# Order of the value products, the second half of the output projection and the norm's scaling in the cross attention stage of an encoder layer

## What is computed

```python
def cross_attn(h, mem_n, wq, wkv, wo):
    q = (h @ wq).reshape(b, t, X_HEADS, X_HEAD_DIM)
    kv = (mem_n @ wkv).reshape(b, m, 2, X_HEADS, X_HEAD_DIM)
    s = jnp.einsum('bqhd,bkhd->bhqk', q, kv[:, :, 0]).astype(f32) * (X_HEAD_DIM ** -0.5)
    p = jax.nn.softmax(s, axis=-1)
    o = jnp.einsum('bhqk,bkhd->bqhd', p.astype(h.dtype), kv[:, :, 1]).reshape(b, t, X_HEADS * X_HEAD_DIM)
    return o @ wo
...
x = x + cross_attn(rmsnorm(x, norm_cross[l]), mem_n, x_wq[l], x_wkv[l], x_wo[l])
gate, up = jnp.split(rmsnorm(x, norm_ffn[l]) @ ffn_w_gu[l], 2, axis=-1)
x = x + (jax.nn.silu(gate) * up) @ ffn_w_down[l]
```

## Time and profile before

| | |
|---|---|
| median of 3 executions | 1893.69 us (1892.82 to 1894.38) |
| the profiled execution's own time | 1895.65 us |
| its span, first to last instruction | 1893.8 us |
| mean granted TensorE clock | 0.958 of full speed |
| PE busy | 1715.6 us, 91% of the span |
| PEld, DVE, ACT, POOL busy | 76%, 39%, 34%, 29% |
| the chain that ended last | PE 80%, DVE 11%, ACT 5% |

### The profile page before, as it was taken

The page is one execution under the profiler, slowest core; times in us unless marked ns, Lnnn a source line. Parts: engine busy times, 40 slices in busy tenths (PEclk is TensorE's granted clock), DMA queues, the critical chain, the costliest instruction groups (busy, mean ns, idle before and its releaser), DMA issues.

```text
span 1893.8 us, 32570 instructions
## 1 busy us (share of the span) xinstructions
PE 1715.6 (91%) x13937; PEld 1430.3 (76%) x13937; DVE 742.0 (39%) x1219; ACT 651.9 (34%) x1218; POOL 552.5 (29%) x498
## 2 busy tenths in 40 slices
PE   7998988899876982988999899999999999999998
PEld 5886777778654771777998687888888888888886
DVE  3104888333265558455223264131233033213316
ACT  4224887322356432433224374221111121211212
POOL 4222763131025324324225102222222222222220
PEclk9998999899878996899999999999999999999999
DMA  5110000021000000001413101111211111111112
GB/s 186 51 60 1 1 1 1 23 71 42 17 1 6 4 4 0 4 4 47 183 51 96 38 1 46 61 41 44 61 48 48 45 50 51 45 56 45 45 45 95
DMA packets 60176, 81.27 MB, mean 43 GB/s; under 512 B 4610, under 2 KB 47776, under 8 KB 60032
## 3 DMA queue, kind: packets, MB, share of 16 engines
q1 hardware_dynamic: 59088, 76.60, 12.6%
q0 software_dynamic: 944, 2.58, 0.5%
HBM read 74.96 MB, written 4.19 MB: 42 GB/s over the span
## 4 chain that ended last, share of the span: by engine, by line
PE 80%; DVE 11%; ACT 5%; issue 2%; DMA 1%; POOL 1%; SPq 0%; DVEq 0%; ACTq 0%
PE PS L1542 13%; PE PS L1543 12%; PE PS L1545 12%; PE PS L1795 7%; PE PS L2139 4%; PE PS L2138 4%; PE PS L2137 4%; PE PS L1555 3%; PE PS L1557 3%; PE PS L1556 3%; PE PS L1653 3%; PE PS L1687 2%; PE PS L1859 2%; PE PS L1679 1%; PE PS L2058 1%
## 5 line engine op out<-in xcount | busy, mean ns | idle before, releaser
L427 POOL TENSOR_TENSOR WL<-RAW,WH 128x512 fp32r<-128x512 f32 x224 | 307.9, 1385 | 913.8 <-ACT WH L589 913.8
L1542 PE MATMUL PS<-HH,WH 128*128 128x512 f32 x1040 | 406.9, 391 | 9.5 <-POOL WL L427 8.0
L1543 PE MATMUL PS<-HL,WH 128*128 128x512 f32 x1040 | 405.7, 390 | 0.0
L589 ACT ACTIVATE WH<-RAW 128x512 fp32r<-128x512 f32 x224 | 138.9, 631 | 594.6 <-PE PS L1545 297.2
L1545 PE MATMUL PS<-HH,WL 128*128 128x512 f32 x1040 | 321.1, 390 | 0.0
L1542 PEld LDWEIGHTS PS<-HH,WH 128*128 128x128 f32 x1040 | 196.1, 189 | 50.6 <-issue 8.3
L1545 PEld LDWEIGHTS PS<-HH,WL 128*128 128x128 f32 x1040 | 195.8, 188 | 40.8
L1543 PEld LDWEIGHTS PS<-HL,WH 128*128 128x128 f32 x1040 | 196.1, 189 | 40.3
L1492 DVE TENSOR_TENSOR FU<-PS,ACTB 128x512 f32<-128x512 f32 x44 | 27.3, 683 | 456.9 <-PE PS L1545 456.9
L2137 PE MATMUL PS<-WH,AH 128*128 128x512 f32 x352 | 136.9, 389 | 0.0
L2138 PE MATMUL PS<-WL,AH 128*128 128x512 f32 x352 | 136.9, 389 | 0.0
(11 more groups left out here) (319 smaller groups left out, 2802.7 us busy)
## 6 DMA issues: line engine op xcount, KB each, us to landing
RAW<-in_ffn_w_gu SPq DMA_DIRECT2D x88, 256.0 KB, 2.8
RAW<-in_w_in SPq DMA_DIRECT2D x48, 256.0 KB, 2.8
RAW<-in_ffn_w_down SPq DMA_DIRECT2D x44, 256.0 KB, 2.6
XT<-in_x SPq DMA_DIRECT2D x8, 512.0 KB, 4.8
RAW<-in_w_out SPq DMA_DIRECT2D x16, 256.0 KB, 2.7
X<-in_x SPq DMA_DIRECT2D x8, 512.0 KB, 8.2
RAW<-in_x_wkv SPq DMA_DIRECT2D x16, 256.0 KB, 2.7
out_x<-FO SPq DMA_DIRECT2D x8, 512.0 KB, 2.6
```

The lines of the kernel that those rows point to most:

```text
L427: pool.tensor_tensor(w_low, RAW[:, p % NRAW], w_high.bitcast(F32), ALU.subtract).then_inc(w_lo, 1)
L589: act.activation(split_at(p)[0], RAW[:, p % NRAW], ACT.Copy).then_inc(w_hi, 1)
L1542: pe.matmul(where(ct, i), wh[:, k, c], ah(kt)[:, t0:t0 + n], start=first and starts(ct, i), stop=False, skip_group_check=True)
L1543: pe.matmul(where(ct, i), wh[:, k, c], al(kt)[:, t0:t0 + n], start=False, stop=False, skip_group_check=True)
```

## The change

Two orders are changed, and no instruction is added or removed. On the PE, values(qb) moves ahead of wo_half(qb-1, 1). On DVE, scale moves from the end of a step to a place behind the next step's c_row_max (so that step qb scales tile qb-2), and c_second(qb) moves ahead of add_wo(qb-1, 1). The ACT program is the same.

```diff
@@ vector engine @@
             for qb in range(NT + 2):
                 if qb + 1 < NT:
                     c_row_max(qb + 1)
+                if qb >= 2:
+                    scale(n3, qb - 2, lambda tt: X[:, tt], lambda tt: XN2[:, tt % 2], BS, BR, GBF[:, :])
                 if 1 <= qb <= NT:
                     add_wo(qb - 1, 0)
                 if qb + 1 < NT:
...
                 if qb >= 2:
                     norm_lo(n3, qb - 2, lambda tt, b: HH[:, 4 * b:4 * b + 4, tt * P:(tt + 1) * P],
                             lambda tt, b: HL[:, 4 * b:4 * b + 4, tt * P:(tt + 1) * P], bank=lambda tt: 6)
-                if 1 <= qb <= NT:
-                    add_wo(qb - 1, 1)
                 if qb < NT:
                     c_second(qb)
                 if 1 <= qb <= NT:
-                    scale(n3, qb - 1, lambda tt: X[:, tt], lambda tt: XN2[:, tt % 2], BS, BR, GBF[:, :])
+                    add_wo(qb - 1, 1)
@@ tensor engine @@
                     turned(qb)
                 if qb >= 2:
                     ffn_tile(qb - 2)
+                if qb < NT:
+                    values(qb)
                 if qb:
                     wo_half(qb - 1, 1)
-                if qb < NT:
-                    values(qb)
```

## The result

| | before | after |
|---|---|---|
| median of all executions, us | 1895.69 (20) | 1902.41 (20) |
| the profiled execution's own span, us | 1893.8 | 1897.9 |
| scores of tile 0 to the first gate product, us | 103.44 | 108.37 |
| one steady step, us | 11.56 | 12.44 |

The ratio of after to before is 1.0032, with a 95% interval of 1.0019 to 1.0046. That is +6.1 us on the 1895.69 us of before, between +3.6 and +8.7. (It is not the ratio of the two medians, which is 1.0035.) The forecast was +4.9 us, and 1898.6 us for the median.

A forecast was written before the change was run, and what follows sets the result against it. It took the PE to bound the kernel, 10.85 us of work and a 0.71 us hole per step. Five steps of +0.85 (+4.25) and start and end (+0.64) gave +4.9 us, a median of 1898.6 us, range 1896.2 to 1903.3.

The forecast's parts named there:

- (a): DVE: row maxima no longer behind scale, could start when scores end, about 1.9 us after those start, cutting the old loop.
- (b): PE: value products directly behind the transposes need their own tile's CPT copy, making a new loop of 12.41 us.
- the old loop: Value products, OH copy, squares, scale, row maxima, residual add, second half, next value products: 11.56 us, the whole step.
- the hole: PE's idle time before the second half in each step of before: 0.71 us.
- The new loop: Second half, residual add, squares, table loads, exponentials, CPT copy, value products, next second half: 12.41 us a step.
- The price that no row of before had in its place: ACT's exponentials right behind their table load: no gap (0.01 us) at the lower bound.
- Rival 4: Page's drain after ACT's table load is real on the new loop: 5 x 1.38 = +6.9 us more, 1905.5; chance 0.03.
- The edges: Start and end of the cross attention stage, outside the five steady steps: together +0.64 us; gate products at 1170.37.
- Rival 1: ACT reaches the exponentials before stat blocks it: step 11.25 us, -0.9 us, 1892.8; chance 0.05.
- Rival 2: The new loop partly looser, release or copy faster: steps of +0.5 to +0.75, 1896.2 to 1897.4; chance 0.10.
- Rival 3: PE clock falls in the new 1.56 us hole before value products: +1.55 us per fall, 1900.2 to 1906.4; chance 0.12.

The follow-up runs named there:

- e3: Against before, only scale moved behind the next row maxima on DVE; step 10.79 us, ratio 0.9982.
- e4: Changed kernel with the root of the norm ahead of the feed-forward part replaced by a copy on ACT; step 11.26 us, ratio to before 0.9983.
- e6: Changed kernel with the squares of the norm ahead of the feed-forward part done twice on ACT; step 13.54 us.
- e1: Against before, only the PE's part: values(qb) ahead of wo_half(qb-1, 1), DVE's order kept; first step 14.04 us, ratio 1.0089.
- e2: Against before, only DVE's part: scale and c_second moved, PE's order kept; step 11.86 us, ratio 1.0018.
- e7: Changed kernel with c_second put back behind the second residual add; step 12.45 us, executed once.
- e9: Kernel with only scale moved, plus the squares of the norm ahead of the feed-forward part done twice on ACT; step 11.48 us.
- e5: Kernel before with the root of the norm ahead of the feed-forward part replaced by a copy on ACT; step 10.75 us, executed once.

## Why the prediction was right

Steps (a) and (b): the row maxima did leave the old loop, and e3 shows that this alone frees 0.8 us a step. That is 0.1 more than the 0.71 that the prediction called the most any reordering could win. It had put the XN transposes at 0.88 us, like those of CP; directly followed by the second half they hold the PE for 0.80 (1115.10 to 1115.90 in e3), so the hole was 0.79. The new loop has the length that was added up, 12.44 against 12.41. Its terms in after, read between 1098.31, 1101.33, 1102.05, 1106.03, 1107.84, 1108.93 and 1110.74: 3.02, 0.72, 3.98, 1.81, 1.09 and 1.81 (the prediction: 3.04, 0.72, 3.96, 1.81, 1.09, 1.79).

The price that no row of before had in its place, the exponentials right behind their load, came out near the lower bound: 1118.49 against 1117.19 + 1.28 = 1118.47. The root's load on the same loop is followed as closely: it ends at 1115.68 + 1.28 = 1116.96, and the root starts at 1116.97. The rule of the Trainium skill (ScalarE: Activation LUTs, What ACT_TABLE_LOAD costs) that a drain of about 1380 ns follows each load does not hold here; with it, by an estimate from that figure, the step would have been 13.8 us. Rival 4 is out.

The edges: gate products +4.89 by the sum, +4.93 measured. The first halves of tiles 6 and 7 wait for the add as worked out. The XN transposes of tile 5 wait 0.26 us for XN, which the sum did not have; it moved little: the value products behind them start 2.22 us after the CP transposes (1154.77 to 1156.99), with 2.16 in the sum.

Rival 1 (ACT keeps clear) is out for the changed kernel; e4 shows it happen, with 11.26 against 11.25, once the table loads are gone. Rival 2 is out. Rival 3 did not come about in the profiled execution, with a hole of 1.43 us: the clock is 1.00 in every stretch of the stage from 1080 us on, and in e6's steady steps too. It came with e1's 3.00 us, so its mechanism was right, and the place wrong. Whether the clock fell in the stage in some of the executions that were not profiled is not shown.

Two things were less good, and one was luck. The waits of the experiments e2 and e6 were put in one place each, and the profile shows them in two; I had followed only the latest wait and not the one behind it, though the sums held. And the time of whole executions varies by more than the effect: the forecast of +4.9 lies inside the measured +3.6 to +8.7, but the ratio does not tell it from +6. That it is about 4.9 rests on the one profiled execution of each kernel, with the step repeated in e7, and on the executions of equal clock, 5.0 us apart.

The luck is in the median. It came out at 1902.41, 3.8 us above the forecast and 0.9 below the upper end of the range, which had been put at 1903.3 for falls of the clock in the new hole. The profiled execution shows no such fall. Of the 3.8 us, 2.0 are there because the median of before rose from 1893.69 (3 executions) to 1895.69 (20); the other 1.8 are within the spread of the executions, and no run shows where they lie.

## What to carry to other kernels

Moving an operation ahead of another on the PE moves the other's result back for everyone who waits for it. Here the second half's add was read by ACT, and behind ACT's wait stood the work for the operation that had been moved ahead: before such a swap, follow each engine's order from the delayed result back to the PE and add the loop up. Work that shows as free, such as a table load in the shadow of a wait, becomes part of the loop when the wait goes. And of a change in several parts each mixture is worth a run: here one part alone brings 0.8 us a step, and the others take it away.

## What was not expected

The opening of the stage, from the scores of tile 0 to those of tile 2, is the same code in all kernels and takes 16.55 us in before, in e1 and in e3, but 16.13 in e9, 17.16 in e2, 17.18 in e6 and 17.64 in e7. The PE has holes of 2 to 3.6 us there, and how long the clock then stays at the lower level differs from one execution to the next (mean granted clock from 1060 to 1080 us: 0.83 in e3, 0.67 in e7):

```profile
1060.00:1080.00 20.00, 11.59 (x42) 0.67 0.14 39
```

The stages ahead vary more: 1060.88 us to the scores of tile 0 in after, 1071.03 in e5, with the same code. This is larger than the effect studied, and why a profiled span, or one execution, cannot carry a verdict of 0.3%.

A hole of 3.00 us behind transposes let the clock fall in every steady step of e1; holes of 0.75 and 1.55 us with eight transposes between them did not in e6, nor did 1.43 us in after, while in an earlier stage it was low 1.5 us after a hole of 1.90 us. In yet another stage of before a hole of 2.83 us, up to 984.01, left it at 1.00 from 982 to 988 us. What decides between these was not tried.
